# Forgetting attention on one Trainium2 core: split values as the stationary tile, split weights streaming past them

## What is computed

```python
def forgetting_attention(q, k, v, log_f):
    ...
        s = jnp.einsum('bqhd,bshd->bhqs', qb, k, preferred_element_type=jnp.float32) * scale
        s = s + (cq[..., :, None] - cum[..., None, :])
        p = masked_softmax(s, kpos[None, :] <= tpos[:, None])
        return jnp.einsum('bhqs,bshd->bqhd', p.astype(v.dtype), v)
...
    q, k, v, f = split_cols(h @ w_in, ODD_SPLITS)
    ...
    return o.reshape(bsz, seq, FOX_W) @ w_out
```

## Time and profile before

| | |
|---|---|
| median of 3 runs | 2446.52 us (2444.91 to 2448.24) |
| the profiled execution | 2448.79 us, of which the span of the trace is 2447.0 us |
| TensorE busy | 2374.6 us (97%) |
| VectorE busy | 1424.7 us (58%) |
| ScalarE busy | 1019.2 us (42%) |
| GpSimd busy | 273.9 us (11%) |
| second layer's attention with its projections | from about 770 to 1003 us of the span |

### The profile page before, as it was taken

How to read it: one execution, slowest core, us unless ns; L and a number is a source line. 1 busy time by engine, 2 the same in 40 slices (tenths; PEclk the granted TensorE clock), 3 DMA queues, 4 the chain that set the end, 5 groups by cost and what they waited for, 6 DMA issues and landing times.

```text
span 2447.0 us, 32007 instructions
## 1 busy us (share of the span) xinstructions
PE 2374.6 (97%) x12074; PEld 1923.7 (79%) x12086; DVE 1424.7 (58%) x2366; ACT 1019.2 (42%) x1732; POOL 273.9 (11%) x260
## 2 busy tenths in 40 slices
PE   8999899999999999999999999989999998999998
PEld 7877788888887888788888866767888776678887
DVE  3545665655655666566556469947533578666333
ACT  3666664322334444443233344444422354444323
POOL 0000111000001000100000236302100233111001
PEclk8999999999999999999999999999999999999999
DMA  4311002333432111133433312111222221102321
GB/s 180 111 54 44 1 19 104 143 133 129 143 133 87 63 59 61 53 121 129 151 125 136 117 66 70 61 35 36 95 96 97 83 70 61 44 27 75 107 95 52
DMA packets 58039, 211.77 MB, mean 87 GB/s; under 512 B 6432, under 2 KB 6560, under 8 KB 57888
## 3 DMA queue, kind: packets, MB, share of 16 engines
q1 hardware_dynamic: 57456, 208.86, 24.9%
q10 hardware_dynamic: 432, 0.85, 0.1%
HBM read 207.60 MB, written 2.10 MB: 86 GB/s over the span
## 4 chain that ended last, share of the span: by engine, by line
PE 83%; DVE 7%; issue 4%; ACT 4%; POOL 1%; DMA 0%; SPq 0%; ACTq 0%; DVEq 0%; POOLq 0%
PE bank L459 76%; PE last_bank L459 4%; PE bank L469 3%; DVE arena L1146 1%; DVE arena L2233 1%; DVE arena L2235 1%; DVE small L832 1%; ACT wparts L567 1%; ACT arena L820 1%; POOL rstd L626 0%; DMA cb_sb<-cb_dram 0%; DVE arena L2568 0%; DVE wparts L571 0%; ACT arena L2141 0%; DVE arena_r L585 0%
## 5 line engine op out<-in xcount | busy, mean ns | idle before, releaser
L459 PE MATMUL bank<-hT,wparts 128*128 128x512 f32 x5520 | 1334.3, 398 | 6.0 <-DMA cb_sb<-cb_dram 3.5
L459 PEld LDWEIGHTS bank<-hT,wparts 128*128 128x128 f32 x5520 | 1033.6, 190 | 237.4 <-issue 23.2
L571 DVE TENSOR_TENSOR wparts<-ring,wparts 128x1024 fp32r<-128x1024 f32 x290 | 367.3, 1267 | 422.1 <-ACT wparts L567 421.7
L459 PE MATMUL bank<-arena_r,wparts 128*128 128x512 f32 x2400 | 550.5, 390 | 0.0
L459 PEld LDWEIGHTS bank<-arena_r,wparts 128*128 128x128 f32 x2400 | 449.4, 188 | 93.8 <-DVE arena_r L601 0.8
L567 ACT ACTIVATE wparts<-ring 128x1024 fp32r<-128x1024 f32 x332 | 348.2, 1049 | 157.6 <-PE bank L459 124.1
L820 ACT ACTIVATE arena<-bank,small 128x128 f32<-128x128 f32 (+3 forms) x192 | 100.9, 526 | 143.6 <-DVE small L832 142.4
L469 PE MATMUL bank<-cf_sb,arena 128*128 128x128 f32 (+1 forms) x816 | 130.3, 276 | 15.3 <-DMA cf_sb<-cf_dram 5.4
L459 PE MATMUL last_bank<-arena 128*128 128x64 f32 x972 | 131.4, 271 | 9.6 <-DVE arena L855 4.3
L459 PEld LDWEIGHTS last_bank<-arena 128*128 128x128 f32 x972 | 122.4, 192 | 18.8 <-issue 12.6
L832 DVE TENSOR_REDUCE small<-bank 128x1 f32<-128x128 f32 (+3 forms) x192 | 93.4, 487 | 56.7 <-PE bank L459 45.1
(11 more groups left out here) (277 smaller groups left out, 2123.3 us busy)
## 6 DMA issues: line engine op xcount, KB each, us to landing
ring<-weights_dram SPq DMA_DIRECT2D x388, 512.0 KB, 3.4
arena<-x_dram SPq DMA_DIRECT2D x4, 512.0 KB, 6.3
out_dram<-arena SPq DMA_DIRECT2D x4, 512.0 KB, 4.0
rot<-rot_dram SPq DMA_DIRECT2D x1, 512.0 KB, 10.9
rot<-rot_dram ACTq DMA_DIRECT2D x1, 512.0 KB, 3.2
cf_sb<-cf_dram SPq DMA_DIRECT2D x1, 416.0 KB, 9.3
cb_sb<-cb_dram SPq DMA_DIRECT2D x1, 264.0 KB, 10.1
vecs<-vec_dram ACTq DMA_DIRECT2D x1, 258.5 KB, 6.3
```

Of the source, the lines that this page charges most:

```text
L459: i = pe.matmul(*args, **kw)
L571: eng.tensor_tensor(wparts[:, slot, 1, :, :], ring[:, p % RAW, :, :], wparts[:, slot, 0, :, :].bitcast(F32), ALU.subtract)\
```

## The change

The product of weights by values is turned round. Values are split into hi and lo when they are copied out of the bank (through `by_head`: ACT writes hi, DVE writes lo) and stand side by side as one 128x128 stationary tile of a head; a ring of three chunks (`VRING`) holds them. The turned weights, split into hi and lo as well, stream past it: per head eight matmuls of 512, 384, 256 and 128 columns, hi and lo each, all into one bank. What comes out is already turned, with the share of v-hi on one half of the partitions and that of v-lo on the other; ACT copies one half across (`swap1`) and DVE adds the two. The weights must be divided by their row sum before they are turned, which POOL does in place (`pool_fox`), and every map is now copied by ACT (hi) and subtracted by DVE (lo). The program of the attention grows from M + 3 to M + 4 steps; the transposes of "ot1" go, and its splits (`act_o1`, `dve_o1`) read from SBUF.

```diff
...
+VRING = 3
+FOX_STEP = SEQ - P
+FOX_PART = FOX_STEP * (NT - 1) + SEQ
...
         def turned_bank(key, n, width=P):
             return banks[key, "nat", n][:, 0:NT * width].rearrange("p (t w) -> p t w", t=NT)
 
+
+        def by_head(key, n):
+            return banks[key, "nat", n][:, :].rearrange("p (t h d) -> p t h d", t=NT, d=DH)
 
...
                     banks.drain((it["key"], "nat", it["n"]), "act_made")
+                elif it["kind"] == "turn" and "low" in it:
+                    act.wait_ge(*filled[it["key"], "nat", it["n"]])
+                    if it["free"] is not None:
+                        act.wait_ge(*it["free"])
+                    act.activation(it["dst"], by_head(it["key"], it["n"]), ACT.Copy)\
+                       .then_inc(*act_made.mark((it["key"], "turned hi", it["n"])))
...
+                elif it["kind"] == "turn" and "low" in it:
+                    dve.wait_ge(*act_made[key, "turned hi", n])
+                    dve.tensor_tensor(it["low"], by_head(key, n), it["dst"].bitcast(F32), ALU.subtract)\
+                       .then_inc(*dve_made.mark((key, "turned", n)))
+                    banks.drain((key, "nat", n), "dve_made")
                 elif it["kind"] == "turn" and "func" not in it:
                     dve.wait_ge(*filled[key, "nat", n])
                     dve.tensor_copy(it["dst"], turned_bank(key, n, it.get("width", P)))\
...
         A = Area()
         q1, k1 = A.take(2, SEQ), A.take(2, SEQ)
         qs1, kh1, kl1 = A.take_r(4, SEQ), A.take_r(4, SEQ), A.take_r(4, SEQ)
-        v1 = A.take(NT, D)
-        onat1 = A.take(NT, D)
-        Pb1, PT1 = A.take(3, SEQ), A.take(3, SEQ)
-        rest, rest2 = PT1[:, 0, :], PT1[:, 1, :]
-        ff, lf, cum = A.take(SEQ), A.take(SEQ), A.take(SEQ)
-        parts3 = A.take16(SEQ)
+        v_at = A.at
+        A.take(VRING * NT * 4 * DH)
+        v1 = arena_r[:, v_at:A.at].rearrange("p (s t b d) -> p s t b d", s=VRING, t=NT, b=4)
+        o1 = A.take(KD, SEQ)
+        turned_at1 = A.at
+        A.take(2 * 2 * FOX_PART)
         vt1 = A.take(2, SEQ)
+        Pb1, swap1 = hv[:, 0:3, :], hv[:, 3, :]
+        early = Area(turned_at1)
+        ff, lf, cum, rest, rest2 = (early.take(SEQ) for _ in range(5))
+        parts3 = rstd[:, 1, 0:SEQ // 2].bitcast(BF16)
         oT1 = Area().take_r(2, KD, SEQ)
+
+        def fox_block(h, part):
+
+            return turned_at1 + (2 * (h % 2) + part) * FOX_PART
+
+        def fox_turned(i, part):
+
+            h, qt = divmod(i, NT)
+            at = fox_block(h, part) + qt * P
+            return arena_r[:, at:at + FOX_STEP * (qt + 1)].rearrange("p (t w) -> p t w", w=FOX_STEP)[:, :, 0:P]
+
+        def fox_moving(h, part, kt):
+
+            at = fox_block(h, part) + FOX_STEP * kt
+            return arena_r[:, at + kt * P:at + SEQ]
 
...
         for c in range(KD):
             items += [item("q1", c, "stack", q1[:, c % 2, :], scale=SCALE, act=act_q1, dve=dve_q1),
                       item("k1", c, "stack", k1[:, c % 2, :], act=act_k1, dve=dve_k1),
-                      item("v1", c, "turn", v1[:, :, c * P:(c + 1) * P])]
+                      item("v1", c, "turn", v1[:, c % VRING, :, 0:4:3, :], low=v1[:, c % VRING, :, 1:3, :],
+                           free=filled["fox", "o", 2 * (c - VRING) + 1] if c >= VRING else None)]
...
                 W = (qt + 1) * P
                 maps.append(dict(
                     qk=[(qs1[:, at, qt * P:W], kh1[:, at, 0:W]), (qs1[:, at, qt * P:W], kl1[:, at, 0:W])], width=W,
-                    masks=[(cstb("selneg")[0:96, h:h + 1].to_broadcast([96, P]), parts3[0:96, 0:W], 0, ()),
-                           (identb, cstb("causal"), qt * P, ())],
-                    v=lambda t, h=h: v1[:, t, h * DH:(h + 1) * DH],
-                    out=onat1[:, qt, h * DH:(h + 1) * DH], gate=None, add=None,
+                    masks=[(cstb("selneg")[0:96, h:h + 1].to_broadcast([96, P]), parts3[0:96, 0:W], 0),
+                           (identb, cstb("causal"), qt * P)],
                     before=(dve_made["q1", c, side, "lo", 1 - side], dve_made["k1", c, side, "lo", 1],
-                            act_made["k1", c, side, "hi", 1 - side]), value=dve_made["v1", "turned", h // 2]))
-
-        fox = softmax_maps("fox", maps, Pb1, PT1, lambda i: small_cols(32, i), lambda i: small_cols(36, i, 6),
-                           [dve_made["lo"]], *POOLS[1:])
-        order = [0, 0, 0] + spread(6, 8) + spread(9, 8) * (KD - 2) + [0] + [1] * (len(maps) + 3)
-        then(alternate(order, project(items[4:], None, None, vt1, vt_free=filled["v1", "nat", 0], pool=POOLS[0], norm=h1), fox))
-        then(turned_parts("ot1", onat1, oT1, [dve_made["fox", "out", 63]]))
+                            act_made["k1", c, side, "hi", 1 - side])))
+
+        M1 = len(maps)
+        S1, O1 = POOLS[1:]
+
+        def mx1(i):
+            return small_cols(32, i)
+
+        def sm1(i):
+            return small_cols(36, i, 6)
+
+        def turned_map(i):
+            W = maps[i]["width"]
+            return banks["fox", "t", i][:, 0:W].rearrange("p (t w) -> p t w", w=P)
+
+        def pe_fox(pe):
+            pe.wait_ge(*dve_made["lo"])
+            for i in range(M1 + 4):
+                if i < M1:
+                    m = maps[i]
+                    for w in m["before"]:
+                        pe.wait_ge(*w)
+                    bank = banks.take(pe, ("fox", "s", i), S1)
+                    for n, (q, k) in enumerate(m["qk"]):
+                        mm(pe, bank[:, 0:m["width"]], lhsT=q, rhs=k, start=n == 0, stop=False)
+                    for n, (a, b, c) in enumerate(m["masks"]):
+                        mm(pe, bank[:, c:c + b.shape[-1]], lhsT=a, rhs=b, start=False, stop=n == 1,
+                           done=("fox", "s", i) if n else None)
+                if 2 <= i < M1 + 2:
+                    j = i - 2
+                    n = j % NT + 1
+                    pe.wait_ge(*pool_made["fox", "scaled", j])
+                    bank = banks.take(pe, ("fox", "t", j), S1)
+                    for t in range(n):
+                        tp(pe, bank[:, t * P:(t + 1) * P], Pb1[:, j % 3, t * P:(t + 1) * P], ident,
+                           done=("fox", "t", j) if t == n - 1 else None)
+                if i >= 6 and i % NT == 2:
+                    h = (i - 6) // NT
+                    c, side = divmod(h, 2)
+                    pe.wait_ge(*dve_made["fox", "lo", NT * h + NT - 1])
+                    pe.wait_ge(*dve_made["v1", "turned", c])
+                    bank = banks.take(pe, ("fox", "o", h), O1)
+                    for kt in range(NT):
+                        values = v1[:, c % VRING, kt, 2 * side:2 * side + 2, :].rearrange("p b d -> p (b d)")
+                        for part in range(2):
+                            last = (kt, part) == (NT - 1, 1)
+                            mm(pe, bank[:, kt * P:SEQ], lhsT=values, rhs=fox_moving(h, part, kt), start=(kt, part) == (0, 0),
+                               stop=last, done=("fox", "o", h) if last else None)
+                yield
+
+        def act_fox(act):
+            for i in range(M1 + 4):
+                if 2 <= i < M1 + 2:
+                    j = i - 2
+                    h, qt = divmod(j, NT)
+                    act.wait_ge(*filled["fox", "t", j])
+                    if qt == 0 and h >= 2:
+                        act.wait_ge(*filled["fox", "o", h - 2])
+                    act.activation(fox_turned(j, 0), turned_map(j), ACT.Copy).then_inc(*act_made.mark(("fox", "hi", j)))
+                if i < M1:
+                    W = maps[i]["width"]
+                    act.wait_ge(*dve_made["fox", "max", i])
+                    if i >= 3:
+                        act.wait_ge(*filled["fox", "t", i - 3])
+                    act.activation(Pb1[:, i % 3, 0:W], banks["fox", "s", i][:, 0:W], ACT.Exp, bias=mx1(i),
+                                   accum_out=sm1(i)).then_inc(*act_made.mark(("fox", "p", i)))
+                    banks.drain(("fox", "s", i), "act_made")
+                if i >= 7 and i % NT == 3:
+                    h = (i - 7) // NT
+                    side = h % 2
+                    act.wait_ge(*filled["fox", "o", h])
+                    if h >= 2:
+                        act.wait_ge(*dve_made["fox", "out", h - 2])
+                    act.activation(swap1[HALF[side], :], banks["fox", "o", h][HALF[1 - side], :], ACT.Copy)\
+                       .then_inc(*act_made.mark(("fox", "swap", h)))
+                yield
+
+        def dve_fox(dve):
+            for i in range(M1 + 4):
+                if i < M1:
+                    W = maps[i]["width"]
+                    dve.wait_ge(*filled["fox", "s", i])
+                    if i >= 3:
+                        dve.wait_ge(*act_made["fox", "p", i - 3])
+                    dve.tensor_reduce(mx1(i), banks["fox", "s", i][:, 0:W], AX.X, ALU.max, negate=True)\
+                       .then_inc(*dve_made.mark(("fox", "max", i)))
+                if 1 <= i < M1 + 1:
```

(42 more changed lines are left out.)

## The result

The kernel got slower: 2475.6 us median of 4 runs (2474.45 to 2476.95) against 2447.4 (2444.91 to 2449.39, 4 runs), ratio 1.0116, 95% interval 1.0098 to 1.0134. The profiled execution took 2476.5 us with a span of 2474.7 (before: 2447.0). I had said 2462.0 with 2442 to 2474: the direction was right, the size too small by 13.6, and the time lies outside the range.

What follows compares the result with a forecast made beforehand. TensorE, busy 97% of the span, was taken as the bound. Saving -12, waits 6 x 1.85 and 5 x 1.4, end +9.3 sum to +15.4 on 2448.8; less 2.3 for the median, 2461.9 us, range 2442 to 2474.

Steps and rivals of the forecast that it cites:

- The saving: TensorE's product of weights by values: 1.0 us less per head, 12 us over twelve heads of six full groups.
- Wait A: TensorE idle before a 512-wide map's transposes, behind addition, stacking, maximum and POOL's division: 1.85 us in each full group.
- rival 2: POOL's division faster than its profile rows, some 0.6 us: +2.4 in all, 2449 us; chance 0.13.
- Wait B: TensorE idle before the values' transposes, waiting for the drain of v: 1.4 us in five groups.
- the end: From the last values' transposes through the last eight maps to the output product, uncovered: +9.3 us.
- The clock falls at the end: Rival: TensorE's granted clock drops in the last stretch and into the output product, 2 to 4 us more, 2466; chance 0.15.
- the two pieces: The woven stage's full groups, +6.1 us net of the saving, and the end, +9.3 us.
- costed at nothing: The values' split on ScalarE and VectorE: hidden beside TensorE's nine projection matmuls, 0 us; without cover 0.6 a chunk.
- The first group: Six projection steps against eight of attention: 0 net, 1.2 us saved and about as much lost, bounds -1 and +1.5.
- no wait: Rival: VectorE and POOL keep ahead, so the change does what it saves, -12 to -16 us, 2433; chance 0.14.
- waits add up: Rival: each lateness shifts the next, panel splits late and projection stopped too, 2475 us and over; chance 0.08.

Runs made afterwards that it cites:

- experiment 5: Changed kernel with transposes, their copies, product run and addition one step later and four weight buffers instead of three: 2446.6 us, ratio 1.0003.
- experiment 4: Changed kernel with only ScalarE's copy across and VectorE's addition of the halves one step later: 2459.6 us, ratio 1.0057.
- experiment 2: Changed kernel without POOL's division, transposes waiting for the exponential alone, output not scaled: 2456.6 us, ratio 1.0046.
- experiment 1: Changed kernel with overwritten junk matmuls put into TensorE's long waits: 2469.9 us, ratio 1.0096.
- experiment 6: Changed kernel, gates' activations behind first projection step: 2474.9 us; or gates' chain ahead of first values' copy: 2469.9, and with experiment 5 2443.5.

## Why the prediction was wrong

**The saving: right where nothing waits.** 1.0 a head was predicted, 0.96 is what it comes to when nothing waits (experiment 5). The run of eight takes 1.31 from its start to that of the next instruction, where the paces added up to 1.21.

**Wait A: right.** Predicted 1.85, measured 1.81 to 1.82 in all six groups, by the chain that was written down. Its two parts are shown by themselves: 0.94 without the addition in the way (said: 1.1), 0.55 without the division. POOL's durations, an estimate from other rows, came out nearly exact:

```profile
L2111 POOL TENSOR_SCALAR hv<-hv,small 128x512 f32<-128x512 f32 x13 | 20.3, 1564 | 33.1 <-DVE small L2089 33.1
...
L2111 POOL TENSOR_SCALAR hv<-hv,small 128x128 f32<-128x128 f32 x14 | 8.4, 603 | 46.9 <-DVE small L2089 46.9
```

That ends rival 2. The Trainium skill (GPSIMD Engine Reference, Engine selection) calls one-input operations on GpSimd roughly line-rate; here 512 columns take it 1564 ns, 2.3 times the 692 that VectorE's lo part of 512 columns takes (L2093), and the measurement decides. The loss beside VectorE's instructions with two SBUF inputs, which the prediction also weighed, is not put to the test: none of the 64 divisions in after's trace overlaps with such an instruction, and those of one size agree within 1%.

**Wait B: mis-sized, and made good by luck.** Predicted 1.4, measured 0.85 twice and 0.33 or 0.34 three times. At full clock the drain of v ended 0.2 sooner than I had added up and TensorE arrived 0.3 later; behind a slow stretch of TensorE the drain is another 0.5 sooner, since VectorE has caught up. The sum had a full group at 27.84 - 2.0 + 1.85 + 1.4 = 29.1, and at full clock it takes 29.0. It fits because something else was left out that costs about as much as B was too large: a wait costs some 0.2 more than its listed idle time. Experiment 5's group of 25.93 has none; with one of 0.94 it is 27.06 (experiment 4), with 0.55 and 0.84 it is 27.7 (experiment 2), with 1.81 and 0.85 it is 28.99 (after). These are 0.2, 0.4 and 0.4 more than 25.93 and the waits.

**The clock: the step that failed.** The prediction let it fall only at the end and only as a rival ("The clock falls at the end", +2 to +4, 0.15), and reckoned the woven stage at full speed. With the clock held by experiment 1 the two pieces that I had summed are as predicted: 174.1 against 173.8, and 28.45 against 28.4 (the end step by step too: from the values' transposes over those of the three 512-wide maps to the output product 3.99, 9.6, 9.1 and 5.8, where the sum had 4.15, 9.3, 8.95 and 6.0). Without it they are 177.2 and 33.3. So the waits were right and their price was not: some 8 us of the miss is the clock, 3.4 in the stage that was reckoned at full speed and 4.9 at the end, where the rival had given it 2 to 4. The evidence was in the sum itself: 1.85 of waiting once in each group and 9 us of idle time in the last eight maps, beside the earlier trace rows, where idle time and a low clock go together.

**The start: "costed at nothing", the second step that failed.** The values' split was set beside TensorE's nine matmuls of P1, and nothing else was asked of it. For the first chunk TensorE has matmuls there too, 24 of them, but what stands behind the split on ScalarE is the gates' chain, which I had not looked at, and which is longer than these 24. Wait 4.81 instead of 0.92, +3.9, shown by moving the chain (experiment 6).

**The first group** cost +0.8, inside the bounds of -1 and +1.5. Some of it is the clock behind the wait of 4.81 (0.83 from 790 to 800 us), so that this was inside is in part luck.

Together: 15.4 predicted, 8.3 more in the two pieces (3.4 and 4.9), 3.9 at the start, 0.8 in the first group, 2.0 behind the output product and -2.75 ahead of the stage, which no edit made, give the span's 27.7. The rivals: "no wait" is refuted in after, and is what experiment 5 makes true within the woven stage; "waits add up" gives the right time for another reason, as the waits were those of the forecast and the projection was not stopped for a panel.

What stays open: why the clock fell behind three of the six waits A and not behind the others (the wait B ahead of the three was 0.85, 0.85 and 0.33, ahead of two of the others 0.34), how much of the last 2.3 us is bank order, and of the 2.0 behind the output product what is not the 1.2 of the low clock there.

## What to carry to other kernels

A step put into a chain of four engines costs by where the chain is short of slack, and the cheap repair is one step more of distance: the same instructions one step later, with a fourth buffer, went from +1.2% to no loss. When a change brings TensorE's first waits to a stage that had none, price the clock with them, in the stage and behind it, and see whether the wait can be shortened (0.94 once a group left it at 1.00 here, 1.81 did not) or filled. For an edit that seems free, read what is queued behind it at the first and the last turn of the loop, where the cover is missing.
